# All expert rounds on unsplit weights: column-tiled float32 products of 64 and 32 slots, a 17-slot weight ring

## The reference

```python
def moe_swiglu(h, w_router, w_gate, w_up, w_down):
    logits = (h @ w_router).astype(jnp.float32)
    top_val, top_idx = lax.top_k(logits, TOP_K)          # TOP_K = 2
    top_w = jax.nn.softmax(top_val, axis=-1)
    gates = jnp.sum(jax.nn.one_hot(top_idx, N_EXPERTS) * top_w[..., None], axis=-2)
    out = jnp.zeros_like(h)
    for e in range(N_EXPERTS):
        out = out + gates[..., e:e + 1] * swiglu(h, w_gate[e], w_up[e], w_down[e])
    return out
```

## Time and profile before

| | |
|---|---|
| median of 3 runs | 1346.24 us (1341.83 to 1346.98) |
| profiled execution | 1346.01 us; its span 1343.9 us; mean granted TensorE clock 0.973 |
| PE busy / PE weight loads | 1252.6 us (93%) / 904.2 us (67%) |
| DVE / ACT / POOL busy | 708.4 us (53%) / 555.1 us (41%) / 104.3 us (8%) |
| moved by DMA | 414.66 MB, mean 309 GB/s |
| chain that ended last | PE 76%, DMA 12%, DVE 5%, SP's queue 3% |

### The profile page before, as it was taken

One profiled execution on the slowest core, in us unless ns is written; L12 is line 12 of the kernel. 1 busy time (PEld: TensorE's weight loads), 2 busy tenths in 40 slices (PEclk: granted clock), 3 DMA queues, 4 the chain that ended last, 5 costly groups with the idle time before them and its releaser, 6 DMA issues.

```text
span 1343.9 us, 17417 instructions
## 1 busy us (share of the span) xinstructions
PE 1252.6 (93%) x6640; PEld 904.2 (67%) x6640; DVE 708.4 (53%) x798; ACT 555.1 (41%) x524; POOL 104.3 (8%) x110
## 2 busy tenths in 40 slices
PE   8899999899997999998799999889999979999985
PEld 7899998778776888633488853368883247887332
DVE  6644445744547788500488830069871027885103
ACT  4434433444433677300467710067760026774001
POOL 0000000000000600010040001022001004000101
PEclk9899999999988999999899999999999999999998
DMA  9855556432234799999999999999999999999994
GB/s 306 288 187 188 188 177 169 125 126 95 94 110 158 252 364 371 338 389 402 394 394 394 401 340 410 402 390 394 394 409 384 406 397 393 394 399 367 395 402 160
DMA packets 175640, 414.66 MB, mean 309 GB/s; under 512 B 8704, under 2 KB 48640, under 8 KB 175488
## 3 DMA queue, kind: packets, MB, share of 16 engines
q1 hardware_dynamic: 174608, 409.79, 82.3%
q0 software_dynamic: 960, 3.80, 0.8%
HBM read 412.52 MB, written 1.05 MB: 308 GB/s over the span
## 4 chain that ended last, share of the span: by engine, by line
PE 76%; DMA 12%; DVE 5%; SPq 3%; issue 2%; ACT 2%; DVEq 0%; ACTq 0%
PE bank L1164 19%; PE bank L1165 19%; PE bank L1166 18%; PE bank L1436 9%; DMA raw_extra<-in_moe_w_down 6%; DMA raw<-in_moe_w_gate 4%; PE bank L1449 3%; SPq L435 2%; PE bank L1394 1%; PE bank L1248 1%; PE bank L1345 1%; DVE w_lo L729 1%; PE bank L1497 1%; ACT w_hi L490 1%; DMA raw<-in_pool_w 1%
## 5 line engine op out<-in xcount | busy, mean ns | idle before, releaser
L729 DVE TENSOR_TENSOR w_lo<-raw,w_hi 128x2048 fp32r<-128x2048 f32 x162 | 369.6, 2294 | 144.0 <-ACT w_hi L490 143.9
L490 ACT ACTIVATE w_hi<-raw 128x2048 fp32r<-128x2048 f32 x162 | 310.0, 1916 | 215.5 <-PE bank L1166 145.3
L1164 PE MATMUL bank<-w_hi,h_hi 128*128 128x512 f32 (+1 forms) x848 | 302.4, 357 | 30.8 <-DVE h_lo L1079 13.8
L1165 PE MATMUL bank<-w_lo,h_hi 128*128 128x512 f32 (+1 forms) x848 | 297.6, 351 | 0.0
L1166 PE MATMUL bank<-w_hi,h_lo 128*128 128x512 f32 (+1 forms) x848 | 297.1, 350 | 0.0
L1164 PEld LDWEIGHTS bank<-w_hi,h_hi 128*128 128x128 f32 x848 | 164.8, 194 | 57.5 <-DVE w_lo L729 17.3
L1166 PEld LDWEIGHTS bank<-w_hi,h_lo 128*128 128x128 f32 x848 | 165.0, 195 | 20.4
L1165 PEld LDWEIGHTS bank<-w_lo,h_hi 128*128 128x128 f32 x848 | 165.0, 195 | 18.8
L1436 PE MATMUL bank<-raw,h_b 128*64 128x512 f32 (+1 forms) x864 | 166.8, 533 | 10.1 <-DMA raw<-in_moe_w_gate 6.1
L729 DVE TENSOR_TENSOR w_lo<-raw_extra,w_hi 128x2048 fp32r<-128x2048 f32 x56 | 131.7, 2358 | 18.0 <-ACT w_hi L490 18.0
L1436 PEld LDWEIGHTS bank<-raw,h_b 128*64 128x64 f32 x864 | 59.8, 137 | 108.2 <-issue 88.8
(11 more groups left out here) (227 smaller groups left out, 1203.8 us busy)
## 6 DMA issues: line engine op xcount, KB each, us to landing
raw<-in_moe_w_up SPq DMA_DIRECT2D x88, 1024.0 KB, 13.1
raw<-in_moe_w_gate SPq DMA_DIRECT2D x84, 1024.0 KB, 12.7
raw_extra<-in_moe_w_down SPq DMA_DIRECT2D x60, 1024.0 KB, 15.6
raw<-in_moe_w_down SPq DMA_DIRECT2D x52, 1024.0 KB, 13.6
raw_extra<-in_moe_w_gate SPq DMA_DIRECT2D x28, 1024.0 KB, 11.1
raw_extra<-in_moe_w_up SPq DMA_DIRECT2D x24, 1024.0 KB, 13.0
raw<-in_ffn_w_gate SPq DMA_DIRECT2D x11, 1024.0 KB, 6.7
raw<-in_ffn_w_up SPq DMA_DIRECT2D x11, 1024.0 KB, 5.2
```

Of the source, the lines that this page charges most:

```text
L490: nc.scalar.activation(w_hi[:, slot, :], raw_slot(source), ACT.Copy).then_inc(hi_ready, 1)
L729: nc.vector.tensor_tensor(w_lo[:, slot, :], raw_slot(source), w_hi[:, slot, :].bitcast(f32), ALU.subtract).then_inc(lo_ready, 1)
L1164: mm(out, a_hi, b_hi, start=first, stop=False)
L1165: mm(out, a_hi, b_lo, start=False, stop=False)
```

## The change

All of the mixture goes unsplit; the dense layer and the attention keep the split.

- **A has 96 slots** instead of 128: 64 "main" and 32 "side". Main slots fill half of the array's columns: two products go side by side, as in B. Side slots fill a quarter: four products stand next to each other, in partitions 0, 32, 64 and 96 onwards (`into_hidden` lines 1382 and 1387, `down` lines 1411 and 1417). B keeps 64 slots.
- **Work units**: an expert has two hidden parts, of 4 chunks of 512 and 4 chunks of 384 columns. Gate and up come in 8 units per part (one block of 128 rows, 2048 or 1536 columns), down in 8 units of two rows per partition and 4 of three. A round has 88 units instead of 84 loads. Stages of A and B are interleaved (`STAGES`).
- **Ring**: 17 MB (`ring`, line 178), with places worked out at build time (`ring_places`). It lies over `raw`, `w_hi`, `w_lo` and the attention's tensors, so its first loads wait for these (`dense_over`). Rows in memory are 8 KB (gate, up and down, first part), 6 KB (gate and up, second) and 12 KB (down, second). The first 17 units (16 of 1 MB, one of 0.75) need no earlier unit of the ring to be used up.
- **ACT and DVE** split nothing in the rounds: ACT does silu, half of the copies and the main rows of `ye`; DVE the multiplications, the other copies, the side rows of `ye` and the sums.
- `X_PAIRS`, the number of further rounds that the table has room for, goes from 4 to 6, which adds four small operations to DVE's routing; the table `iota_b` (two operations) is gone.

```diff
-X_PAIRS = 4
-CAP = 128
-CAP_B = 64
+X_PAIRS = 6
+MAIN = 64
+SIDE = 32
+CAP = MAIN + SIDE
+CAP_B = MAIN
+CHUNKS = 4
+SG_WIDTH = (512, 384)
+STAGES = (("A", "gate", 0), ("A", "up", 0), ("A", "gate", 1), ("A", "down", 0), ("A", "up", 1), ("B", "gate", 0),
+          ("A", "down", 1), ("B", "up", 0), ("B", "gate", 1), ("B", "down", 0), ("B", "up", 1), ("B", "down", 1))
...
+def unit_size(kind, name, sg, i):
+    if name == "down":
+        return (2 + sg) * D
+    return CHUNKS * SG_WIDTH[sg]
...
-            for j in range(2):
-                lo(MOE_U0 + j)
...
+                def into_hidden(kind, name, sg, blocks):
+                    n, h, to = SG_WIDTH[sg], {"A": h_a, "B": h_b}[kind], {"gate": 0, "up": 3}[name]
+                    for k in blocks:
+                        w = landed_unit(first_unit(kind, name, sg) + k)
+                        for c in range(CHUNKS):
+                            t = c % 2
+                            step = mm(bank[to + c // 2][t * MAIN:(t + 1) * MAIN, 0:n], h[:, k, 0:MAIN],
+                                      w[:, c * n:(c + 1) * n], start=(k == 0), stop=(k == KB - 1))
+                            if kind == "B" and c >= 2:
+                                step.then_inc(expert_used, 1)
+                        for c in range(CHUNKS if kind == "A" else 0):
+                            mm(bank[to + 2][c * SIDE:(c + 1) * SIDE, 0:n], h[:, k, MAIN:CAP], w[:, c * n:(c + 1) * n],
+                               start=(k == 0), stop=(k == KB - 1)).then_inc(expert_used, 1)
...
+                def down(kind, sg):
...
+                            for t in range(2):
+                                step = mm(bank[6][t * MAIN:(t + 1) * MAIN, :],
+                                          aT[:, 4 * (c // 2) + j, (c % 2) * MAIN:(c % 2 + 1) * MAIN],
+                                          w[:, b * D + t * HALF:b * D + (t + 1) * HALF], start=first, stop=last)
...
+                            for q in range(CHUNKS if kind == "A" else 0):
+                                step = mm(bank[7][q * SIDE:(q + 1) * SIDE, 0:2 * P],
+                                          aT[:, 8 + j, c * SIDE:(c + 1) * SIDE],
+                                          w[:, b * D + q * 2 * P:b * D + (q + 1) * 2 * P], start=first, stop=last)
...
+                tokens_ready(0)
+                into_hidden("A", "gate", 0, range(KB))
+                pe.wait_ge(acc_done, p * 8 + 2)
+                into_hidden("A", "up", 0, range(KB))
...
+                into_hidden("B", "up", 1, range(KB))
+                transposed("B", 1, 8)
+                aT_ready(6, 4)
+                down("B", 1)
+                pe.wait_ge(ye_act, p * 4 + 4)
+                scatter(MAIN, gselT_b, (3, 4, 5, 6))
```

More of the change, by code:

```diff
@@ L24 @@
 F_EXP = 3584
-N_EG = F_EXP // HALF
 EPS = 1e-6
@@ L60, with select @@
 WARM = (32, 30, 10, 12, 28, 4)
-def select(eng, ops, chain, before, gpos, gpos_next, step, gate, sel, sel2, gsel, iota, ready,
+def select(eng, ops, chain, before, slots, gpos, gpos_next, step, gate, sel, sel2, gsel, iota, ready,
            ready_count, done, ALU):
@@ L273, in trunk @@
             landed.append(on_slot[u % RAW_SLOTS])
[L276 to L296, removed]
         def u_gate(g):
@@ L466, in of_table, with first_down @@
+            def first_down(u):
+                return u < N_UNITS and UNITS[u][1:] == ("down", 0, 0)
             def of_table(at):
                 return sp.value_load(rtab_i[0:1, bass.ds(at, 1)], min_val=0, max_val=E - 1)
-            expert_a(0, 0)
+            ahead_units = [u for u in range(N_UNITS) if place_held_by(u) < 0]
+            for u in ahead_units:
+                for at in range(PLACE[u] // UNIT, (PLACE[u] + unit_size(*UNITS[u]) - 1) // UNIT + 1):
+                    dense_over(at)
+                fetch(u, source(UNITS[u], 0))
@@ L472, in _ @@
             with sp.Fori(0, pairs) as p:
-                expert_b(p, of_table(p + (1 + PAIRS + X_PAIRS)))
-                with sp.If(p < pairs - 1):
-                    expert_a(p, of_table(p + 2), 1)
+                expert = {"A": of_table(p + 1), "B": of_table(p + (1 + PAIRS + X_PAIRS))}
+                for u in range(len(ahead_units), N_UNITS):
+                    weights = source(UNITS[u], expert[UNITS[u][0]])
+                    if not first_down(u):
+                        freed = place_held_by(u + 1 if first_down(u + 1) else u)
+                        sp.wait_ge(expert_used, p * PAIR_USED + USED[freed])
+                    fetch(u, weights)
+                with sp.If(p < pairs - 1):
+                    following = of_table(p + 2)
+                    for u in ahead_units:
+                        weights = source(UNITS[u], following)
+                        sp.wait_ge(expert_used, p * PAIR_USED + USED[place_held_by(u)])
+                        fetch(u, weights)
             for tb in range(TB):
@@ new lines, in _ @@
+                act_of("A", 0, 0, 0)
+                aT_of("A", 0, 0)
+                gathered(p, 1, h_b, MAIN)
+                act_of("A", 1, 3, 3)
+                aT_of("A", 1, 3)
+                ve.wait_ge(expert_used, used_by(p, "A", "down", 1))
+                for q in range(CHUNKS):
+                    nc.vector.tensor_copy(ye[MAIN:CAP, q * 2 * P:(q + 1) * 2 * P],
+                                          bank[7][q * SIDE:(q + 1) * SIDE, 0:2 * P]).then_inc(ye_dve, 1)
+                accumulate(p * 8, (0, 1, 2, 6))
```

613 lines of the change are left out of this document (256 added, 357 removed).

## The result

| | before | changed |
|---|---|---|
| median | 1346.35 us (1341.83 to 1349.53, 20 runs) | 1350.7 us (1346.06 to 1357.0, 20 runs) |
| profiled execution: time, span | 1346.01, 1343.9 us | 1357.0, 1354.9 us |
| second profile of the changed kernel | | 1349.49, 1347.4 us |

The ratio is 1.0038, 95% interval 1.0027 to 1.0048: the changed kernel is 0.4% slower, where 0.9% faster was forecast. The wide range (1272 to 1372 us) held it, the sign did not. One run of all those behind this document, of 3749.35 us in experiment 10, stands apart from the rest and is left out of its ratio.

What follows compares the result with a forecast made beforehand. DMA bound the kernel, PE close behind; afterwards PE. First product 432.6 + 4 x 222.5 - 2.3 + 11 + 1 = 1332.3 us of span, with 2.1 outside 1334.4, so 1334 us, 0.9% faster; range 1272 to 1372.

Steps and rivals of the forecast that it cites:

- The start: Before the first expert: without two splits and `iota_b`, routing's copy at about 415.3 us, first product at about 432.6 instead of 436.69.
- The step: PE's products in the experts: a pair of records, 512 columns through both halves at full clock, starts every 0.43 us.
- the four abreast: Expert A's side slots: four quarter-tile products run side by side in 2 steps, 36.1 us a round.
- not four abreast: Rival, expert A's quarter products: 18.1 us a round per further step, two abreast gives 1478 us; chance 0.21.
- Term 2: Expert A's bursts: 60 alternations between half and quarter tiles a round at 0.26 us each, 15.6 us.
- without a price: Rival, expert A: half and quarter tiles follow each other free, time about 1284 us as loads bind again; chance 0.21.
- the turn of the round: From expert B's scatter into the next round: scatter 3.63 us, return to the loop's start 2.26.
- one microsecond in the whole program for a low clock: Added in the sum: 1 us for a low clock at the start, from 0.99 over 115 us.
- The waits without cover: Per round, after the last up product about 1.5 us, after the last down product 1.4; with the return 5.2 together.
- The loads: DMA in the rounds: longer rows land at 409 to 420 GB/s, lower bound 380, and no longer set the end.
- end +0.55: After the last scatter: 11 us to the end of the span, where the kernel before took 12.5.

Runs made afterwards that it cites:

- experiment 10: Changed kernel with groups of four units (two in down), next gather cut into expert B's idle places, 12 dummy products behind the first gather: 1283.33 us, ratio 0.9528.
- experiment 2: Changed kernel with expert A's four quarter-tile products per unit replaced by two half-tile products, computing something else: 1282.26 us, ratio 0.9528.
- experiment 8: Changed kernel with half-tile, then quarter-tile products over four units (two in down): 1297.2 us; also with the next gather cut into idle places: 1284.73 us.
- experiments 1: Changed kernel with half-tile products of two units, then the quarter-tile products of both, down likewise: 1305.45 us, ratio 0.9698 to the kernel before.
- experiment 7: Changed kernel with the gather of the next slots cut in three and put into PE's idle places at expert B's end: 1333.94 us, ratio 0.9918.

## Why the prediction was wrong

- **The start was right**, as near as the runs allow. Forecast first product 432.6, measured 431.55; the routing's copy, forecast at 415.3, starts at 415.25. That the copy agrees to 0.05 us is luck: from profile to profile it moves between 413.13 and 419.17.
- **The step and the four abreast were right**: 2.57 us for six steps (experiment 2), 0.86 for eight more quarter records (experiment 8). The rival "not four abreast" is out. The rule cited with it, the Trainium skill, TensorE: Matmul & The Clock Gate, Measured speedup vs the span model, would have given 2.5 steps by my estimate; the trace has 2.0 in the stream, so for four tiles of float32 records in an unbroken stream the measurement decides (no run here tried three).
- **Term 2 had the right mechanism and was 9% small.** Forecast 0.26 us an alternation, measured 0.28 to 0.29. Over 240 alternations 0.025 us more are 6.0 us. The rival "without a price" is out: experiments 1, 2 and 8 took 38, 60 and 46 alternations away, and rounds became 11.1, 17.5 and 13.5 us shorter. The rule that speaks for the price, the Trainium skill, TensorEngine Tiling (Array Packing), Key Properties (a change of tiling mode drains the engine), agrees with the trace in that every change costs time, and the trace adds the figure, 0.14 us a change.
- **The term that failed most is the turn of the round.** The prediction had the scatter 3.63, the return 2.26 and then a unit at full speed, and one microsecond in the whole program for a low clock. From the scatter's start to the second unit of the next round it is 12.15, 11.02 and 12.09 us (651.07 to 663.22, 878.46 to 889.48, 1104.73 to 1116.82) against 3.63 + 2.26 + 2.86 = 8.75: 3.0 us more a turn, 9.0 in three. Of these 7.0 are in the first units (5.46, 4.61 and 5.55 instead of 2.86), 2.0 in the scatter and the return together. The first unit of all took 4.28 us (431.55 to 435.83), 1.4 more. I took the 2.26 us of the earlier trace rows over and did not ask at which clock PE comes back, though the trace of the kernel before showed it. Right behind that return, from its chain:

```profile
671.31 0.43 PE bank L1164
...
673.70 0.23 PE bank L1164
```

The first products after the return take 0.43 us each, and 0.23 from 673.5 on; the window 669.80 to 673.30 has a granted clock of 0.52. It is so at two of that kernel's three turns (after 667.53 and after 1114.7, not after 890.9), about 1.6 us each. The granted clock in the earlier trace rows, 0.98 in the two rounds that hold these turns and 1.00 in the other, points there too. In the changed kernel all three turns pay, and more: the order of instructions quoted ahead of the prediction showed that no product stood between the last down product and the scatter any more.
- **Neither term alone turns the sign.** 1334.4 and 9.0 for the turns is 1343.4, 1334.4 and 6.0 for the alternations is 1340.4, both under the 1346 of the kernel before; together they make 1349.4. A saving of 12 us had stood on two terms that were too small by 15.
- **The waits without cover** were right: 1.5 and 1.4 forecast, 1.5 (3.1 + 2.8 us in four rounds) and 1.3 measured.
- **The loads** were right in kind, better in size: not binding, 416 to 425 GB/s where the forecast took 409 to 420.

The sum, against the second profile: 1332.3 forecast span, start -1.05, alternations +6.0, turns +9.0, first unit +1.4 less the 1.0 foreseen, end +0.55 (11.55 from the scatter's end to the span's), together 1347.2; measured 1347.4.

**Where the expected gain went.** Compared with the kernel before, 28.4 us of waits for loads and 5.1 us of the start (one profile of each kernel) are gone, and 10.2 us in which PE waited at the turns for the gathered slots; 11.1 us of waits for the copies are new. Expert A costs PE 16 x 2.86 + 16 x 2.22 + 28 x 1.58 = 125.5 us a round instead of 114.2, 45 us more in all. Of the 125.5 the alternations are 17.1: the change paid with them, 68 us in four rounds, for what it had won. That they could have been had for a quarter of it is experiment 8. What PE does in the 0.14 us of a change no run shows.

## What to carry to other kernels

Count the alternations between tile sizes, not only the columns: put products of one size together, as far as the store of loaded weights allows, here four units of 17 (two in down) and not eight (four in down). When a change lifts one bound, price the idle places on the other engine anew, first of all those that the old bound had hidden, with the clock at which the engine comes back from them. Fill idle places with work that has to be done anyway; dummies cost here what they gave.

## What the runs showed of the hardware

- A change between 64-column and 32-column tiles costs 0.13 to 0.14 us each way (0.28 to 0.29 for both), with 512 and with 384 columns, in bursts of eight records and of 32.
- Four 32-column float32 products of different weights run in the time of two 64-column ones, 0.86 us for 512 columns, inside a burst (32 records in 3.57 us).
- Rows of 6 to 12 KB land at 421 GB/s and rows of 1.5 to 4 KB, read in another order, at 390, with as many bytes, issues and places.
- At the turn of a round PE comes back at the 1.2 GHz level for about 3 to 6 us, in the kernel before at two of three turns. Covering the waits ahead of the return did not prevent it (experiment 7), 24 dummy products in them did at two of three turns, with a shorter return (1.7 to 2.0 instead of 2.4 to 3.0 us where the scatter ran at full clock). Why the one and not the other stays open.
- Ahead of the first expert the low clock fell, from profile to profile and with no edit at that place, either on the gather (6.8 to 7.0 us instead of 3.8) or on the products behind it.
